# Seven products in place of eight for the down projections of a channel mixer, and one accumulation bank for its up projections

## What is computed

```python
D_MODEL = 1024; SEQ = 256; DEPTH = 2; D_FF = 2816
def swiglu(x, w_in, w_out):
    gate, up = jnp.split(x @ w_in, 2, axis=-1)
    return (jax.nn.silu(gate) * up) @ w_out
...
x = layer_norm(ALPHA * x + 0.5 * swiglu(x, ffn1_w_in[l], ffn1_w_out[l]), ...)
x = layer_norm(ALPHA * x + y, ...)                     # y: mixer AB (l = 0) or C (l = 1)
x = layer_norm(ALPHA * x + 0.5 * swiglu(x, ffn2_w_in[l], ffn2_w_out[l]), ...)
```

## Time and profile before

| | us |
|---|---|
| median of 3 runs (989.84 to 990.45) | 990.25 |
| the profiled execution | 989.61 |
| its span, first to last instruction | 988.1 |
| TensorE busy | 976.5 (99%) |
| VectorE busy | 716.0 (72%) |
| ScalarE busy | 501.0 (51%) |
| mean granted TensorE clock, 1 is 2.4 GHz | 0.998 |

### The profile page before, as it was taken

The page is one execution under the profiler, slowest core; times in us unless marked ns, Lnnn a source line. Parts: engine busy times, 40 slices in busy tenths (PEclk is TensorE's granted clock), DMA queues, the critical chain, the costliest instruction groups (busy, mean ns, idle before and its releaser), DMA issues.

```text
span 988.1 us, 13756 instructions
## 1 busy us (share of the span) xinstructions
PE 976.5 (99%) x5012; PEld 824.7 (83%) x5012; DVE 716.0 (72%) x980; ACT 501.0 (51%) x559; POOL 35.9 (4%) x63
## 2 busy tenths in 40 slices
PE   9999999999999999999999999999999999999996
PEld 7888888888888888888888888878888888888885
DVE  5686667795879665667787575789999967565665
ACT  6663544336647544543544343348998535344430
POOL 0100000000210000000000000000100100000000
PEclk9999999999999999999999999999999999999999
DMA  8687655553657756564666555725233656656521
GB/s 298 222 276 249 208 168 200 174 174 125 232 199 235 240 176 212 169 207 136 199 227 199 183 191 191 232 81 199 86 129 128 213 194 231 213 169 207 167 96 42
DMA packets 129255, 184.70 MB, mean 187 GB/s; under 512 B 5953, under 2 KB 104785, under 8 KB 129089
## 3 DMA queue, kind: packets, MB, share of 16 engines
q1 hardware_dynamic: 126032, 173.56, 52.5%
q0 software_dynamic: 2624, 10.11, 2.9%
q10 hardware_dynamic: 560, 0.52, 0.2%
HBM read 183.13 MB, written 1.05 MB: 186 GB/s over the span
## 4 chain that ended last, share of the span: by engine, by line
PE 92%; DVE 3%; ACT 3%; DMA 1%; issue 1%; POOL 0%; DVEq 0%; SPq 0%; ACTq 0%
PE psum L1551 24%; PE psum L1525 17%; PE psum L1527 17%; PE psum L1526 17%; PE psum L1555 12%; DMA raw<-in_ffn_w_in 1%; PE psum L1992 1%; ACT w_hi L430 1%; PE psum L1520 1%; PE psum L1668 1%; PE psum L1978 1%; DVE w_lo L843 0%; DVE xT L871 0%; ACT psum L769 0%; ACT L769 0%
## 5 line engine op out<-in xcount | busy, mean ns | idle before, releaser
L843 DVE TENSOR_TENSOR w_lo<-raw,w_hi 128x2048 fp32r<-128x2048 f32 x161 | 367.4, 2286 | 40.8 <-ACT w_hi L430 40.1
L1551 PE MATMUL psum<-xT,w_hi 128*128 128x512 f32 x1024 | 358.4, 395 | 0.0
L430 ACT CAST w_hi<-raw 128x2048 fp32r<-128x2048 f32 x161 | 304.2, 1909 | 27.9 <-DMA raw<-in_ffn_w_in 17.6
L1555 PE MATMUL psum<-xT,w_lo 128*128 128x256 f32 x1024 | 275.4, 279 | 0.0
L1551 PEld LDWEIGHTS psum<-xT,w_hi 128*128 128x128 f32 x1024 | 190.0, 188 | 41.4
L1555 PEld LDWEIGHTS psum<-xT,w_lo 128*128 128x128 f32 x1024 | 192.8, 188 | 5.5
L934 DVE TENSOR_REDUCE ffn_tok<-psum 128x256 f32<-128x512 f32 x128 | 82.4, 686 | 151.0 <-PE psum L1551 151.0
L1525 PE MATMUL psum<-w_hi,xT 128*128 128x512 f32 x447 | 177.8, 398 | 1.0 <-DVE xT L864 0.7
L1527 PE MATMUL psum<-w_hi,xT 128*128 128x512 f32 x447 | 174.4, 390 | 0.0
L1526 PE MATMUL psum<-w_lo,xT 128*128 128x512 f32 x447 | 174.3, 390 | 0.0
L464 ACT ACTIVATE ffn_tok<-ffn_tok 128x256 f32<-128x256 f32 x64 | 26.8, 418 | 231.8 <-DVE ffn_tok L934 231.8
(11 more groups left out here) (192 smaller groups left out, 677.3 us busy)
## 6 DMA issues: line engine op xcount, KB each, us to landing
raw<-in_ffn_w_in SPq DMA_DIRECT2D x170, 512.0 KB, 4.8
raw<-in_ffn_w_out SPq DMA_DIRECT2D x88, 512.0 KB, 4.0
raw<-in_c_w_in SPq DMA_DIRECT2D x32, 512.0 KB, 4.6
raw<-in_ab_w_in SPq DMA_DIRECT2D x16, 512.0 KB, 4.8
raw<-in_ab_w_o SPq DMA_DIRECT2D x8, 512.0 KB, 3.7
raw<-in_c_w_o SPq DMA_DIRECT2D x8, 512.0 KB, 3.7
ln_gb<-in_ln_gain POOLq DMA_DIRECT2D x6, 512.0 KB, 6.7
ln_gb<-in_ln_bias POOLq DMA_DIRECT2D x6, 512.0 KB, 7.3
```

The lines of the kernel that those rows point to most:

```text
L430: nc.scalar.copy(w_hi[:, n % RING], raw[:, slot]).then_inc(hi_ready, 1)
L843: nc.vector.tensor_tensor(w_lo[:, n % RING], raw[:, n % RAW], w_hi[:, n % RING].bitcast(F32), ALU.subtract).then_inc(lo_ready, 1)
L1551: return nc.tensor.matmul(dst, w_hi[:, slot, cs], xT_both[:, kk].rearrange("p a f -> p (a f)"), start=kk == 0, stop=kk == KB - 1)
L1555: return nc.tensor.matmul(dst[:, 0:SEQ], w_lo[:, slot, cs], xT_hi[:, kk], start=False, stop=False)
```

## The change

The down projections of chunks 0 to 8 are no longer 8 triples but 7: the hidden values and the w_out unit are taken as 2 x 2 blocks, sums and differences of blocks are formed (Winograd's form of Strassen's scheme), and the seven products accumulate over the nine chunks in seven banks (PROD). Chunks 9 and 10 go through `down` as before. Of the w_out unit three blocks are split plainly (`split_plain_hi`, `split_plain_lo`, 128 x 1536) and four sums are formed by DVE (`weight_sums`, 128 x 512 each) and split (`split_sums_hi`, `split_sums_lo`, 128 x 2048). ACT copies the transposed hidden values from PSUM to SBUF (`hidT_copy`), DVE forms four sums (`hidden_sums`, 128 x 128 each), ACT and DVE split seven blocks (`hid_blocks_hi`, `hid_blocks_lo`, 128 x 896).

With seven banks taken, one bank, G[0], is left for the up projections and the transposes of chunks 0 to 9. `project_fold` is gone: chunks 2 to 9 use `project`, with four transposes, both token tiles through G[0] one after the other. At the end of a mixer `sums_out` and two copies on ACT take four product banks to SBUF and `sums_in` adds them to x. A raw buffer of w_out is free when `weight_sums` is done. The w_hi and w_lo rings have fixed places: two pairs for A and B, one for the plain part, one for the sums.

The diff, cut to its core:

```diff
+        PROD = [bank[5], bank[3], bank[2], bank[1], bank[0], bank[6], bank[7]]
...
+            def split_plain_hi(n, i=None):
+                landed(n, i)
+                freed(plain_free[nth[n] - 1], i)
+                nc.scalar.copy(w_hi[:, PLAIN, 0:1536], raw[:, n % RAW, 512:]).then_inc(plain_hi, 1)
...
+            def split_sums_hi(name, n, i=None):
+                act.wait_ge(w_sums, nth[n] if i is None else i * 2 + nth[n])
+                freed(sums_free[nth[n] - 1], i)
+                nc.scalar.copy(w_hi[:, SUMS], SUM_PLACES[name].rearrange("p a f -> p (a f)")).then_inc(sums_hi, 1)
...
+            def hidT_copy(name, c, src):
+                f = SILUS[name]
+                act.wait_ge(hidT_done, c + (NH * f + 1))
+                if f or type(c) is not int or c:
+                    act.wait_ge(hidT_lo, c + NH * f)
...
+                nc.scalar.copy(hid_blocks[:, 0:512], src).then_inc(hidT_copied, 1)
...
+            def hid_blocks_hi(name, c):
+                f = SILUS[name]
+                act.wait_ge(hid_sums, c + (N_PROD * f + 1))
+                if f or type(c) is not int or c:
+                    act.wait_ge(sums_used, c + N_PROD * f)
+                nc.scalar.copy(hT_hi_flat[:, 0:896], hid_blocks[:, P:]).then_inc(hidT_hi, 1)
...
+                        n, c = s0 + 7 + 3 * par, i * 2 + (2 + par)
+                        split_plain_hi(n, i)
+                        hidT_copy(name, c - 1, G[0])
+                        split_hi(n + 1, i)
+                        hid_blocks_hi(name, c - 1)
+                        ffn_silu(name, 0, c, G[0])
+                        split_sums_hi(name, n, i)
+                        split_hi(n + 2, i)
+                        ffn_silu(name, 1, c, G[0])
                 n, c = s0 + FFN_UNITS - 1, NC - 1
+                split_hi(n - 1)
+                hidT_copy(name, c - 1, G[0])
+                act.wait_ge(hidT_copied, N_COPY * (f + 1))
+                act.wait_ge(sums_used, N_PROD * (f + 1))
+                nc.scalar.copy(hT_hi[:, 0], hid_blocks[:, 0:512]).then_inc(hidT_hi, 1)
+                factor = NORMS[name][1]
+                nc.scalar.activation(kept[0], PROD[0], ACT.Copy, scale=factor).then_inc(copied_out, 1)
+                nc.scalar.activation(kept_last, PROD[4], ACT.Copy, scale=factor).then_inc(copied_out, 1)
...
+            def weight_sums(name, n, part, i=None):
+                nth_now = nth[n] if i is None else i * 2 + nth[n]
+                w = raw[:, n % RAW].rearrange("p (a f) -> p a f", a=4)
+                b12, b11, b22, b21 = (w[:, a] for a in range(4))
+                t1, t2, t3, t4 = (SUM_PLACES[name][:, a] for a in range(4))
+                if part == 0:
+                    dve.wait_ge(plain_hi, nth_now)
+                    nc.vector.tensor_tensor(t1, b12, b11, ALU.subtract).then_inc(w_step1, 1)
+                    nc.vector.tensor_tensor(t3, b22, b12, ALU.subtract)
+                else:
+                    dve.wait_ge(w_step1, nth_now)
+                    nc.vector.tensor_tensor(t2, b22, t1, ALU.subtract).then_inc(w_step2, 1)
+                    dve.wait_ge(w_step2, nth_now)
+                    nc.vector.tensor_tensor(t4, b21, t2, ALU.subtract).then_inc(w_sums, 1)
+            def split_sums_lo(name, n, i=None):
+                dve.wait_ge(sums_hi, nth[n] if i is None else i * 2 + nth[n])
+            def split_sums_lo(name, n, i=None):
+                dve.wait_ge(sums_hi, nth[n] if i is None else i * 2 + nth[n])
+                nc.vector.tensor_tensor(w_lo[:, SUMS], SUM_PLACES[name].rearrange("p a f -> p (a f)"),
+                                        w_hi[:, SUMS].bitcast(F32), ALU.subtract).then_inc(sums_lo, 1)
+            def hidden_sums(name, c):
+                f = SILUS[name]
+                a = hid_blocks.rearrange("p (a f) -> p a f", f=P)
+                a21, a11, a22, a12, s1, s2, s3, s4 = (a[:, b] for b in range(8))
+                dve.wait_ge(hidT_copied, c + (N_COPY * f + 1))
+                nc.vector.tensor_tensor(s1, a21, a22, ALU.add).then_inc(hid_step1, 1)
+                nc.vector.tensor_tensor(s3, a11, a21, ALU.subtract)
+                dve.wait_ge(hid_step1, c + (N_PROD * f + 1))
+                nc.vector.tensor_tensor(s2, s1, a11, ALU.subtract).then_inc(hid_step2, 1)
+                dve.wait_ge(hid_step2, c + (N_PROD * f + 1))
+                nc.vector.tensor_tensor(s4, a12, s2, ALU.subtract).then_inc(hid_sums, 1)
+            def hid_blocks_lo(name, c):
+                dve.wait_ge(hidT_hi, c + (SILUS[name] * NH + 1))
+                nc.vector.tensor_tensor(hT_lo_flat[:, 0:896], hid_blocks[:, P:], hT_hi_flat[:, 0:896].bitcast(F32),
...
+                        n, c = s0 + 7 + 3 * par, i * 2 + (2 + par)
+                        split_plain_lo(n, i)
+                        hidden_sums(name, c - 1)
+                        weight_sums(name, n, 0, i)
+                        hid_blocks_lo(name, c - 1)
+                        weight_sums(name, n, 1, i)
+                        ffn_hidden(name, 0, G[0], c * 2, ffn_tok[:, 1, 0])
+                        split_lo(n + 1, i)
+                        split_sums_lo(name, n, i)
+                        ffn_hidden(name, 1, G[0], c * 2 + 1, ffn_tok[:, 1, 1])
                         split_lo(n + 2, i)
-                        fold_hid_lo(name, c, par)
                 n, c = s0 + FFN_UNITS - 1, NC - 1
                 if name == BEFORE_AB:
                     head_constants()
+                split_lo(n - 1)
+                dve.wait_ge(hidT_hi, NH * f + c)
+                nc.vector.tensor_tensor(hT_lo[:, 0], hid_blocks[:, 0:512], hT_hi[:, 0].bitcast(F32), ALU.subtract
+                                        ).then_inc(hidT_lo, 1)
+                sums_out(name)
                 split_lo(n)
+                ffn_hidden(name, 0, G[0], c * 2, ffn_tok[:, 1, 0])
+                sums_in(name)
                 split_lo(n + 1)
-                dve.wait_ge(hidT_lo, c + SILUS[name] * NH)
-                ffn_hidden(name, 0, G[0], c * 2, ffn_tok[:, 1, 0])
+                last_hidT(name, 0)
                 split_lo(n + 2)
-                last_hidT(name, 0)
-                split_lo(n + 3)
                 norm_stats(name, 0)
                 ffn_hidden(name, 1, G[1], c * 2 + 1, ffn_tok[:, 1, 1])
                 norm_gain(name, 0)
                 last_hidT(name, 1)
...
+            def sums_out(name):
+                f, factor = SILUS[name], NORMS[name][1]
+                dve.wait_ge(copied_out, 2 * f + 1)
+                nc.vector.scalar_tensor_tensor(out=kept[1], in0=PROD[5], scalar=factor, in1=kept[0],
+                                               op0=ALU.mult, op1=ALU.add).then_inc(moved_out, 1)
+                dve.wait_ge(moved_out, 2 * f + 1)
+                nc.vector.scalar_tensor_tensor(out=kept_both, in0=PROD[6], scalar=factor, in1=kept[1],
+                                               op0=ALU.mult, op1=ALU.add).then_inc(moved_out, 1)
+            def sums_in(name):
+                f = SILUS[name]
+                dve.wait_ge(copied_out, 2 * f + 2)
+                nc.vector.tensor_tensor(x_tok[:, 1, 512:], x_tok[:, 1, 512:], kept[0], ALU.add)
+                step(nc.vector.tensor_tensor(x_tok[:, 1, 0:512], x_tok[:, 1, 0:512], kept[1], ALU.add))
+                nc.vector.tensor_tensor(x_tok[:, 1, 0:512], x_tok[:, 1, 0:512], kept_last, ALU.add)
+                step(nc.vector.tensor_tensor(x_tok[:, 0, 0:512], x_tok[:, 0, 0:512], kept_last, ALU.add))
+                dve.wait_ge(moved_out, 2 * f + 2)
+                x0 = x_tok[:, 0].rearrange("p (h f) -> p h f", h=2)
+                step(nc.vector.tensor_tensor(x0, x0, kept_both.unsqueeze(1).to_broadcast([P, 2, 512]), ALU.add))
...
+            def products(name, n, i, c, which, used=None, first=False, last=False):
+                for p in which:
+                    slot, part = B_OF[p]
+                    nth_now = nth[n] if i is None else i * 2 + nth[n]
+                    pe.wait_ge(plain_lo if slot == PLAIN else sums_lo, nth_now)
+                    ts, cs = slice(A_OF[p] * P, (A_OF[p] + 1) * P), slice(part * 512, (part + 1) * 512)
+                    ins = three_passes(PROD[p], hT_hi_flat[:, ts], hT_lo_flat[:, ts], w_hi[:, slot, cs],
+                                       w_lo[:, slot, cs], first, last and p in ALONE)
+                if used is not None:
+                    ins.then_inc(used, 1)
+            def hidden_T(name, readings, dst, tiles=(0, 1)):
...
+            def loop_chunk(name, s0, i, par, c, last=False):
+                f, n = SILUS[name], s0 + 5 + 3 * par
+                hid = 2 * f * NC
+                pe.wait_ge(hidT_copied, c + N_COPY * f)
+                project(n, i, 0, G[0])
+                pe.wait_ge(hidT_lo, c + NH * f)
+                products(name, n + 2, i, c - 1, (0, 1), None, False, last)
+                pe.wait_ge(hid_ready, c * 2 + (hid + 1))
+                project(n, i, 1, G[0])
```

(8 more changed lines are left out.)

340 lines of the change are left out of this document (166 added, 174 removed).

## The result

The changed kernel takes 1029.22 us (median of 4, 1027.86 to 1035.45) against 990.29 for the one before: 1.041 times as long, 95% interval 1.036 to 1.045. The forecast was 1019 within 1003 to 1034. Direction and range held; the sum was 10 us short, and two terms of it were wrong.

What follows compares the result with a forecast made beforehand. The prediction took TensorE's issue to bound the kernel. From 989.6, loops -13.0, entries +31.7 (including the clock's 2) and ends +10.5 gave 1018.8; it said 1019, range 1003 to 1034.

Steps and rivals of the forecast that it cites:

- Loops, -13.0: Loops of all mixers: 16.5 us saved over 32 chunks, less 1.6 for late weight loads and 1.9 for table reloads.
- the read of the bank: Loop, between t0 and t1: two products cover reading the single bank; a late weight load loses about 0.05 a chunk.
- The reloads: Loops of F0 and F1: ACT's function-table reload before `hidT_copy` makes it 0.3 late, six turns, 1.9 us.
- DVE's spare time: Loop, from t1's multiply to the next chunk's t0 multiply: DVE has 0.65 us to spare, the thinnest cover.
- F0's entry, +11.1: F0, before chunk 2: split, angles, sine, reload and copy in sequence delay its start from 36.33 to 47.4.
- The clock, +2: After F0's 8.9 us gap TensorE runs 4 us at half speed, costing 2 us; bounds 0 and 5.
- Rival 3: Besides F0's gap, eight gaps of 2.9 to 3.7 us halve the clock, about 2 each: 16, 1035; chance 0.12.
- F1, F2 and F3: Entries of these mixers' loops: sums, table work and copies delay TensorE by +7.8, +7.3 and +3.5 us.
- The gap of 3.5 in F2's chunk 2: F2's entry: `lower_bound` parts on DVE delay chunk 1's `hid_blocks_lo`, so TensorE waits another 3.5 us.
- The waits for the sums: Entries, before product 4: DVE delivers `sums_lo` late, after splitting A2 and multiplying; 3.3 us lost in F3.
- The ends, +10.5: Ends of F0, F1 and F2: late load, DVE's additions and another split cost 3.5 each; F3's additions hide.

Runs made afterwards that it cites:

- e6: Changed kernel with products 0 and 1 of the loop moved behind t1's projection, so nothing covers the bank's read: 1065.89 us.
- e2: Like e1, with the entries' table work (angles, exponential arguments, bound parts, sine, exponentials) moved into the loop's written-out first turns: 1008.12 us.
- e8: e2 plus two unused subtractions of 512 columns a chunk on DVE, between the weights' sums and t0's multiply: 1027.19 us.
- e1: Changed kernel with POOL issuing AB's five table loads after the fourth lo unit instead of the fifth: 1020.32 us.
- e4: Changed kernel with DVE making t0's last hidden values' lo part before the five additions at a mixer's end: 1028.20 us.
- e5: e2 with the five additions at a mixer's end on POOL instead of DVE: 1011.80 us.
- e7: e5 with the four sums of chunk 0's w_out rows also made on POOL in each mixer: 1018.81 us.
- e11: e9 with conversion of C's constants moved into F1's loop, bound work a chunk later, and bound inputs and F1's and F2's weight sums relocated: 987.64 us.
- e3: Changed kernel with entries reordered: chunk 1's transposes and product 0 before product 4, and the sums' lo part before A2's on DVE: 1036.73 us.
- e10: e2 with the five additions at the ends spread over DVE's idle places, two, one and two: 1002.25 us.
- e9: e10 with entries filled too: chunk 0's weight sums in DVE's idle time, ACT's rounding earlier, remaining tables and bounds moved: 993.89 us.

## Why the prediction was right, and where it was wrong

- **Loops, -13.0.** The mechanism is right, and 2.4 more came back than counted. A chunk takes 16.12 to 16.13, where the sum had 16.14 and another 0.05 for the read of the bank. That read is covered in full: t1 starts 6.80 to 6.82 after t0, and 5.44 + 1.36 is 6.80 (e6 gives the price without cover). The reloads cost 1.4 in all for 1.9 (e2 is without them). DVE's spare time is 0.55 by the trace and 0.8 by e8, for 0.65. No run takes the seven products and the other form of the projection apart; their shares of the 0.5 a chunk are the prediction's.
- **F0's entry, +11.1.** The step that failed is "then the angles" right behind A2 and B2: it took the tables as landed. Their wait counts units, and the prediction had renumbered the units for the splits but not for POOL. That is 8.2 us, and e1 shows it. From the angles on, the chain was right to 0.4 us. The change lowers the number in POOL's second wait, for other tables, and leaves that of the first as it was.
- **The clock, +2.** Mis-sized by 5: it costs 2.9 in F0, 2.6 in F2 and 1.6 in F3. Rival 3 named the mechanism and gave it 0.12; of its eight places three were hit in the profiled run, and its price of 2 us for each is near that of most falls (1.6 to 1.7, and 2.6 in F2). It should have been a term of the sum, at half weight.
- **F1, F2 and F3.** Chunk 2 starts 25.2, 20.9 and 22.0 after chunk 0's t1, for 25.1, 20.8 and 20.8; F3's surplus is its half clock. The gap of 3.5 in F2's chunk 2 is 3.37. The waits for the sums were there (3.06 to 3.07 for 3.3; 2.69 in F0).
- **The ends, +10.5.** The three gaps make 7.7 for 9.6. The mechanism, DVE's additions ahead of the lo part, was only half of it: e4 shows that behind the lo part DVE's work in sum is the next bound. AB's and C's +0.9 and +0.5, which the sum had as 0, are not explained. AB takes 83.4 and 83.3, nearly as before, where POOL makes F0's additions (e5, e7), which points to DVE's work there; no run isolated it.
- **The sum.** 8.2 and 5 on top and 1.4 in AB and C, against 1.9 less at the ends and 2.4 less in the loops: 10.3, and the table by stages shows 9.8. That the time fell into the range was in part luck. It stayed in the range because the range reached to rival 3, and the larger part of what filled it, the late tables, was a mechanism that no rival named.

Whether the change itself is bad is answered by e11: with as many matmuls and DVE instructions as the changed kernel (4520 and 1204), it is 2.4 us faster than before. The 41.6 us between e11 and the changed kernel were places in an order, a few places in SBUF, one counter and the clock. The loops alone promise 16.5; the rest of e11 still keeps 14 of it.

## What to carry to other kernels

A change that saves TensorE work in a loop pays for its latencies at every entry and end of it; count DVE's idle places there from the trace first, since a new order without a free place only moves the wait (e3, e4), while the same steps in idle places bring time back (e10, e9). When the kinds that a semaphore counts change, go through every wait on it on every engine, loads above all. And a load's landing belongs in the chain: the engine that frees its place issues it.

## What the runs showed of the hardware

- **Short gaps and the clock.** Over the traces of all kernels here, 64 gaps of TensorE of 2.4 to 3.5 us: 40 were followed by the half clock, 24 were not, and the same gap drew a fall in one kernel and none in the next (before product 4 of F2: 3.06 to 3.09 us in nine kernels, five falls). The fall came 2 to 5 us after the gap's start, often when TensorE worked again, and mostly lasted 3.4 us, which costs some 1.6 us. These kernels are also less steady: 7.6 us lie between fastest and slowest with the changed kernel and 7.6 with e9, at most 1.1 before. In e9 the fastest execution has a mean granted clock of 0.998 and the slowest 0.993, so the clock is a part of it; that it is all of it is not shown. With the Trainium skill (TensorE: Matmul & The Clock Gate, Part 1), which has a rested TensorE at half rate, the traces agree; the return, which the trace of before did not show, took 6 us of work after the long gap.
- **POOL beside DVE** (e5, e7): an addition of 512 columns takes POOL 1.25 us alone and 3.3 beside DVE's splits; DVE's split of 2048 columns takes up to 3.40 for 2.28 and its addition of 256 columns 1.5 for 0.42.
